# Two v stages become one: half of the second token tile's experts by fetched rows and VectorE additions, on one Trainium2 core

## The reference, cut to what matters

```python
def blk(args):                      # hx: tokens x 2048, e: expert numbers, gt: gates
    hx, e, gt = args
    act = jax.nn.gelu(jnp.einsum('nd,nhkd->nhk', hx, expert_u[e]), approximate=False)
    return jnp.einsum('nhk,nhkd->nd', gt * act, expert_v[e])
```

## Time and profile before

| | |
|---|---|
| time, median of 3 runs (lowest, highest) | 3488.04 us (3487.63, 3488.38) |
| profiled execution, span from first to last instruction | 3487.5 us |
| busy: PE, PEld, DVE, ACT, POOL | 99%, 83%, 63%, 51%, 10% |
| moved by DMA | 638.58 MB, mean 183 GB/s |
| granted TensorE clock, mean | 0.998 |

### The profile page before, as it was taken

How to read it: one execution, slowest core, us unless ns; L and a number is a source line. 1 busy time by engine, 2 the same in 40 slices (tenths; PEclk the granted TensorE clock), 3 DMA queues, 4 the chain that set the end, 5 groups by cost and what they waited for, 6 DMA issues and landing times. The chain is left out here.

```text
span 3487.5 us, 50169 instructions
## 1 busy us (share of the span) xinstructions
PE 3450.4 (99%) x20098; PEld 2893.0 (83%) x20098; DVE 2194.8 (63%) x2937; ACT 1766.6 (51%) x2613; POOL 347.2 (10%) x215
## 2 busy tenths in 40 slices
PE   8999999999999999999999999999999999999999
PEld 7777777787999998888888888887788877788887
DVE  4777765765666686555555565555788885555454
ACT  5563444334444785444444444444655654444863
POOL 0000000000499100000000000000122210000000
PEclk9999999999999999999999999999999999999999
DMA  6554533565445555555555666555543435455444
GB/s 235 203 198 156 174 138 130 187 232 212 161 183 182 174 168 183 215 190 185 191 213 184 240 231 228 189 185 180 191 148 138 148 140 202 168 194 190 145 150 164
DMA packets 111214, 638.58 MB, mean 183 GB/s; under 512 B 17770, under 2 KB 23690, under 8 KB 39224
## 3 DMA queue, kind: packets, MB, share of 16 engines
q1 hardware_dynamic: 106696, 622.98, 50.0%
q0 software_dynamic: 4336, 13.14, 1.2%
HBM read 611.10 MB, written 21.54 MB: 181 GB/s over the span
## 5 line engine op out<-in xcount | busy, mean ns | idle before, releaser
L222 DVE TENSOR_TENSOR lo_w<-ring,hi_w 128x1024 fp32r<-128x1024 f32 x500 | 612.4, 1225 | 862.7 <-ACT hi_w L216 854.2
L216 ACT CAST hi_w<-ring 128x1024 fp32r<-128x1024 f32 x540 | 567.1, 1050 | 946.3 <-DMA ring<-in_wstream 920.6
L224 DVE TENSOR_TENSOR lo_w<-ring,hi_w 128x1024 fp32r<-128x1024 f32 x500 | 612.4, 1225 | 0.0
L217 ACT CAST hi_w<-ring 128x1024 fp32r<-128x1024 f32 x540 | 564.4, 1045 | 0.0
L639 PE MATMUL PS<-hi_w,both_x 128*128 128x512 f32 (+2 forms) x1520 | 500.2, 399 | 4.9 <-DVE RKV L1651 3.0
L2074 PE MATMUL PS<-hi_w,hi_g 128*128 128x512 f32 x1024 | 404.0, 395 | 2.0 <-issue 2.0
L2667 PE MATMUL PS<-hi_w,both_x 128*128 128x512 f32 x1232 | 401.3, 401 | 4.1 <-PEq L1968 1.9
L2074 PE MATMUL PS<-lo_w,hi_g 128*128 128x512 f32 x1024 | 403.4, 394 | 0.0
L2074 PE MATMUL PS<-hi_w,lo_g 128*128 128x512 f32 x1024 | 403.2, 394 | 0.0
L2048 PE MATMUL PS<-both_x,hi_w 128*128 128x256 f32 x2176 | 390.5, 281 | 3.1 <-POOL lo_w L224 3.1
L639 PEld LDWEIGHTS PS<-hi_w,both_x 128*128 128x128 f32 x1520 | 285.2, 189 | 78.3 <-issue 12.3
(11 more groups left out here) (579 smaller groups left out, 5272.4 us busy)
## 6 DMA issues: line engine op xcount, KB each, us to landing
ring<-in_wstream SPq DMA_DIRECT2D x540, 1024.0 KB, 4.8
other_G<-staged SPq DMA_DIRECT2D x32, 256.0 KB, 6.0
hot<-other_G SPq DMA_DIRECT2D x8, 1024.0 KB, 7.0
gates_dram<-gst POOLq DMA_DIRECT2D x8, 512.0 KB, 4.6
x_dram<-x SPq DMA_DIRECT2D x2, 2048.0 KB, 11.8
x<-x_dram SPq DMA_DIRECT2D x2, 2048.0 KB, 9.3
prev<-RKV POOLq DMA_DIRECT2D x6, 508.0 KB, 5.1
x<-in_x SPq DMA_DIRECT2D x4, 512.0 KB, 8.9
```

Source lines behind the costliest of these rows:

```text
L216: a.copy(hi_w[s][:, 0:HALF], ring[s][:, 0:HALF]).then_inc(S(f"hi{s}"), 1)
L217: a.copy(hi_w[s][:, HALF:UNIT], ring[s][:, HALF:UNIT]).then_inc(S(f"hi{s}"), 1)
L222: v.tensor_tensor(lo_w[s][:, 0:HALF], ring[s][:, 0:HALF], hi_w[s][:, 0:HALF].bitcast(F32), ALU.subtract)
L224: v.tensor_tensor(lo_w[s][:, HALF:UNIT], ring[s][:, HALF:UNIT], hi_w[s][:, HALF:UNIT].bitcast(F32), ALU.subtract)\
```

## The change

The order of the stages becomes u of the experts from 64 on (called u_b: both tiles, unpaired), u of those below 64 (u_a, unpaired), then one v stage of 128 units. Its first 64 units are the experts from 64 on, for both tiles, as before. Its last 64 are those below 64, for the first token tile alone: 12 matmuls of 512 columns each in place of 24.

Note that the diff's `v_expert(p)` calls the last 64 units sparse, and that `HK + i` in the layout of the stream are the experts from 64 on.

For the second tile the experts below 64 go another way. In 128 steps, one per pick, GpSimd fetches by indirect DMA for each of the 128 tokens the v row of that pick (`fetch`: 128 x 2048 float32 into one of three, later four, later three buffers), and VectorE adds it to x of that tile with its weight in one scalar_tensor_tensor (`add_row`). Picks of experts from 64 on are out of the bounds of the fetch and are skipped; their weight is 0. The weight is the gate times the gelu, which GpSimd fetches one word per token from DRAM (`cell`: 128 indirect DMAs of 128 words, into a raw array that starts at 0; VectorE multiplies 32 of them at a time, `weigh`, at ticks 9, 12, 36 and 38 of u_a). So the gelus of u_b (whose name in DRAM is act_dram) are stored unit by unit by SyncE (`keep_act`, 128 KB each). Additions 0 to 53 stand in u_a, one per unit from unit 10; 54 to 127 in the first 61 units of v.

What moves besides. lo_w: GpSimd makes it for all 64 units of u_b, VectorE for all of u_a, and in v GpSimd for even and VectorE for odd units. G: VectorE copies one half of each burst to GG (`copied`) in place of copy and product, ScalarE stages the other half for the first tile only (16 of 32). In u_a VectorE multiplies each unit's gelu into GG (`times_a`). The gelus of the first tile's last 64 v units are loaded from DRAM (`load_act`, six slots, 64 KB each), as is a table of G for them (tab_b, 4 MB in one DMA before the first v unit), and VectorE multiplies them (`times_b`, with a strided read of the table). GG's layout changes, so that one unit's 256 values are contiguous. `u_sum`, `product`, `product_back`, `late` go, and so do the save and reload of x in the middle and four of the final eight additions to x (the second tile's four stand after the 64th v unit). The u parts of both halves are unchanged in what they compute.

The diff, cut ("..." marks what is left out):

```diff
-STREAM = [("w_in", 19), ("br_b", 2), ("br_a", 2), ("w_out", 4), ("wq", 4), ("u0", 16), ("v0", 16), ("u1", 16), ("v1", 16),
+STREAM = [("w_in", 19), ("br_b", 2), ("br_a", 2), ("w_out", 4), ("wq", 4), ("u_b", 16), ("u_a", 16), ("v", 32),
           ("a_in", 16), ("a_out", 4), ("kv", 8), ("b_in", 8), ("b_out", 4)]
...
+HK = PK // 2
+def v_expert(p):
+    return p >= HK, p % HK
...
+    act_dram = scratch("act_dram", (HK, P, T))
...
+    rows = {"x0": x[:, 0, :], "h1": lanes(hot1), "h2": lanes(hot2), "g0": GG[:, 0:8, :].rearrange("p i t -> p (i t)")}
+    x1 = x[:, 1, :]
...
+    ADD0, ADDS_U = 10, HK - 10
+    ADDS_V = PK - ADDS_U
+    SPAN_V = LAST_A - 2
+    adds_u = lambda i: [i - ADD0] if i >= ADD0 else []
+    adds_v = lambda p: list(range(ADDS_U + ADDS_V * min(p, SPAN_V) // SPAN_V, ADDS_U + ADDS_V * min(p + 1, SPAN_V) // SPAN_V))
...
+            with sp.Fori(0, STEADY // SLOTS) as j:
+                for s in range(SLOTS):
+                    sp.wait_ge(S("unit_used"), j * SLOTS + (W0 + s + 1))
+                    sp.dma_start(ring[s][:], wst[ds(j * SLOTS + (W0 + SLOTS + s), 1)].rearrange("a p f -> p (a f)"))\
+                        .then_inc(S(f"landed{s}"), 16)
+                    sp.wait_ge(S("gelu_free"), j * SLOTS + (s + 5))
+                    sp.dma_start(act_dram[ds(j * SLOTS + s, 1)].rearrange("a p t -> p (a t)"), act_early[:, s, :])\
+                        .then_inc(S(f"act_out{s}"), 16)
...
+            refill(GROUP["u_a"], 1)
+            sp.wait_ge(S("G"), NB)
+            for s in range(SLOTS):
+                sp.wait_ge(S(f"act_out{s}"), 16 * (HK // SLOTS))
+            for k in range(AHEAD):
+                load_act(k)
+            refill(GROUP["u_a"] + 1, HK // SLOTS - 1)
             for p in range(2):
...
+                sp.wait_ge(S(f"other_out{p}"), 8 * NB0)
+            sp.dma_start(tab_b, other_G).then_inc(S("tab_in"), 16)
+            for p in range(VB):
+                refill_unit(VB + p)
+                sparse, k = v_expert(p)
+                if sparse and k + AHEAD < HK:
+                    load_act(k + AHEAD)
...
-                    if paired:
-                        nc.tensor.matmul(PS[:, s, :].rearrange("p (a c) -> p a c", a=2), hi_w[s][:, k * P:(k + 1) * P], both_x[:, :, k, :],
-                                         start=k == 0, stop=False)
-                        m = nc.tensor.matmul(PS[:, s, 0:T], lo_w[s][:, k * P:(k + 1) * P], hi_x[:, k, :], start=False, stop=k == KC - 1)
-                        continue
...
+            def v_half(g, s, last=False):
+                t.wait_ge(S(f"lo{s}"), g + (GROUP["v"] + 1))
+                t.wait_ge(S("g_lo"), g * 4 + (s + 1))
+                for c in range(4):
+                    m = v_products(g, s, 0, c, False, last)
+                    if last and c < 3:
                         m.then_inc(S("v_bank"), 1)
...
+            for w in range(2 * HK):
+                for j in at_unit(w):
+                    if j < NB0:
+                        stage(j)
+                    if j + 2 < NB:
+                        gate(j + 2)
...
+                if SLOTS <= w < HK + SLOTS:
+                    a.wait_ge(S(f"act_out{w % SLOTS}"), 16 * (w // SLOTS))
+                elif w >= HK + SLOTS:
+                    a.wait_ge(S("gg_mul"), w - HK - SLOTS + 1)
+                a.wait_ge(S("unit_used"), W0 + w + 1)
+                a.activation(act_stage(w), PS[:, w % SLOTS, 0:T], ACT.Gelu).then_inc(S("gelu_free"), 1)
...
+            for p in range(VB):
+                if p + 2 < VB:
+                    high(p + 2)
+                hi(VB + p + SLOTS - 1)
...
-            for w in range(AT_UNIT[0]):
+            def fetch(s):
+                n = row_of[s]
+                if row_before[s] >= 0:
+                    g.wait_ge(S("added"), row_before[s] + 1)
+                elif n == "g0":
+                    g.wait_ge(S("unit_used"), W0 + VB + 8)
+                elif n in ("h1", "h2"):
+                    g.wait_ge(S("G"), NB)
+                g.indirect_dma_start(rows[n], None, dram["v_rows"], bass.IndirectOffsetOnAxis(ap=row_at[:, s:s + 1], axis=0),
+                                     bounds_check=HK * P - 1, oob_is_err=False).then_inc(S(f"row_{n}"), 16)
+            def cell(s):
+                g.indirect_dma_start(raw[:, s:s + 1], None, act_cells, bass.IndirectOffsetOnAxis(ap=cell_at[:, s:s + 1], axis=0),
+                                     bounds_check=HK * P * T - 1, oob_is_err=False).then_inc(S(f"cells{s // CELLS}"), 16)
+            def lo(w):
                 split_lo(g, (W0 + w) // SLOTS, w % SLOTS)
+            for w in range(HK):
+                lo(w)
+                if w == 48:
+                    g.wait_ge(S("row_at"), 1)
+                    fetch(0)
+            for s in (1, 2):
+                fetch(s)
+            for s in range(SLOTS):
+                g.wait_ge(S(f"act_out{s}"), 16 * (HK // SLOTS))
+            for s in range(2 * CELLS):
+                cell(s)
+            for i in range(ADD0, HK):
+                for s in fetches(i):
+                    fetch(s)
+                at = 2 * CELLS + 4 * (i - ADD0)
+                for s in range(at, min(at + 4, PK)):
+                    cell(s)
+            lo(VB)
+            lo(VB + 2)
+            for p in range(VB):
+                for s in fetches(HK + p):
+                    fetch(s)
+                if p % 2 and p + SLOTS - 1 < VB:
+                    lo(VB + p + SLOTS - 1)
...
-                if AT_UNIT[0] <= w < 4 * HK + SLOTS:
+                if HK <= w < VB or VB <= w < 2 * VB and w % 2 or 2 * VB <= w < 2 * VB + SLOTS:
                     split_lo(v, (W0 + w) // SLOTS, w % SLOTS)
...
+            def copied(j):
+                if j == 0:
+                    for s in range(SLOTS):
+                        v.wait_ge(S(f"act_out{s}"), 16 * (AT_UNIT[0] // SLOTS))
                 v.wait_ge(S("G"), j + 1)
-                v.wait_ge(S("gelu_free"), m + 4)
                 b = 4 + 2 * (j % 2)
                 got = PS[:, b:b + 2, :].rearrange("p b (n i) -> p (b n) i", i=PK)
-                o = GG[:, 8 * j:8 * j + 8, 0:m]
-                v.tensor_copy(late_, got[:, :, m:HK])
-                v.tensor_tensor(o, o, got[:, :, 0:m], ALU.mult).then_inc(S("G_product"), 1)
...
+                v.tensor_copy(GG[:].rearrange("p i t -> p t i")[:, 8 * j:8 * j + 8, :], got[:, :, HK:PK])
+                v.drain().then_inc(S("G_copy"), 1)
...
+            def add_row(s):
+                n = row_of[s]
+                if s == 0:
+                    v.wait_ge(S("x_again"), 16)
+                v.wait_ge(S(f"row_{n}"), 16 * row_turn[s])
+                v.scalar_tensor_tensor(out=x1, in0=rows[n], scalar=weight[:, s:s + 1], in1=x1, op0=ALU.mult, op1=ALU.add)
+                v.drain().then_inc(S("added"), 1)
+            def times_a(i):
+                v.wait_ge(S("gelu_free"), HK + i + 5)
+                v.tensor_tensor(GG[:, i, :], GG[:, i, :], act_stage(HK + i), ALU.mult).then_inc(S("gg_mul"), 1)
+            def times_b(k):
                 if k == 0:
+                    v.wait_ge(S("tab_in"), 16)
+                v.wait_ge(S(f"act_in{k % AHEAD}"), 16 * (k // AHEAD) + 16)
+                o = act_b[:, k % AHEAD, :]
+                v.tensor_tensor(o, o, tab_b[:, :, k], ALU.mult).then_inc(S("gb_mul"), 1)
+            def low(p):
+                sparse, k = v_expert(p)
+                v.wait_ge(S("g_hi"), p + 1)
+                src, w = (act_b[:, k % AHEAD, :], P) if sparse else (GG[:, k, :], T)
+                v.tensor_tensor(lo_g[:, p % SLOTS, 0:w], src, hi_g[:, p % SLOTS, 0:w].bitcast(F32), ALU.subtract).then_inc(S("g_lo"), 1)
...
+            for i in range(ROUTED, HK):
+                for j in at_unit(i):
+                    copied(j)
+                    if j + 2 < NB:
+                        build(j + 2)
+            lo(HK)
+            lo(HK + 1)
+            for i in range(HK):
+                lo(HK + i + SLOTS - 2)
+                if i:
+                    times_a(i - 1)
+                if i in (9, 12, 36, 38):
+                    weigh((9, 12, 36, 38).index(i))
+                for s in adds_u(i):
+                    add_row(s)
...
+            times_a(HK - 1)
+            v.drain()
+            for p in range(VB):
+                if p + 3 < VB and v_expert(p + 3)[0]:
+                    times_b(v_expert(p + 3)[1])
+                    v.drain()
+                if p + 2 < VB:
+                    low(p + 2)
+                if p < VB - 1:
+                    lo(VB + p + SLOTS - 1)
+                for s in adds_v(p):
+                    add_row(s)
```

398 lines of the change are left out of this document (186 added, 212 removed).

## The result

The changed kernel takes 3589.51 us (median of 4 runs, 3587.56 to 3592.66) against 3488.21 us (3487.63 to 3496.78) for the kernel before, a ratio of 1.0284 with a 95% interval of 1.027 to 1.0299: 101 us slower where 27 us less were forecast, and outside the range of 3370 to 3550. Nothing in the sum hangs on it.

What follows compares the result with a forecast made beforehand. TensorE, busy 99% of the span, was taken as the bound. Terms: v stages 41 us gained, first u stage 9 lost, second u stage 5 lost, the rest 0; -27 on 3488.0 gave 3461 us, range 3370 to 3550.

Steps and rivals of the forecast that it cites:

- part 7, the cells: Second u stage: 128 single-cell indirect DMAs plus fetches on GpSimd, 0.94 us each, cost 0; upper bound 130 us.
- Part 2, half units: The 64 one-tile v units: 3.75 us each, 240 us in all; bounds 3.4 and 4.4 us.
- The ring of 14.8 us: Half units: refill, cast, lo_w with holds, then TensorE take 14.8 us per turn of four units, a quarter being 3.7.
- Part 3, whole units: Whole v units with additions: GpSimd's lo_w holds VectorE off, 6.75 us per unit, 428 us; bounds 5.54 and 7.5.
- The rival without any hold: v stage: additions not held off, whole units 5.54 us, total 3358, or 3379 to 3388; chance 0.15.
- Part 4, bursts: First u stage: GpSimd's lo_w and VectorE's one-hots hold each other off, 9 us lost; bounds 0 and 35 us.
- Part 6: Transfers: row fetches, 4 MB table at the first v unit and activation loads cost 0; table up to 5 us.
- Parts 1 and 5: v units: TensorE alone would save 177 us; second u stage: unpaired units at 5.69 us, 5 us lost.
- Part 8: Ends of stages: final additions into x split 4 and 4, reload and save of x go; cost 0.
- the third rival: Half units: TensorE's granted clock falls to the 0.51 level, 4.4 us per unit, 42 us more, 3503; chance 0.08.
- the second rival: Second u stage: GpSimd's indirect DMAs become the bound; at c = 1.5 us each, 57 us, 3518; chance 0.25.
- the forecast's own case: Whole kernel, no rival true: 3461 us, own range about 3425 to 3505; chance 0.50.

Runs made afterwards that it cites:

- Edit 1: Changed kernel with 32 single cells first, then two per unit (before 64, then four), weights formed at units 9, 40, 50, 62: 3527.7 us, ratio 1.0105.
- edit 2: Changed kernel with VectorE making lo_w for all 128 v units and GpSimd for none: 3434.9 us, ratio 0.9834.

## Why the prediction was wrong, step by step

- **The step that failed: part 7, the cells, put at 0.** The price per indirect DMA was taken from the earlier trace rows, 0.94 us, as busy time of a direct DMA. It is 0.99 busy and 1.30 from start to start, as the rows above show, 1.43 in the mean of the 64 in a row and 1.6 in the ticks, where one in each lies beside an addition. "At 0.94: 0" became 62 us. The rival had it right, with its place, both of its terms and its break-even (1.29 us). With the measured prices the part's own formulas give 65 x 1.43 - 69 = 24 us for the 64 in a row (22 measured, in one unit) and 16 x (8.0 - 5.69) = 37 for the ticks (about 41). Edit 1 removes the cause and gives 62 us back. What no term had is that TensorE's clock falls with its waits, 17 of the 62 us.
- **Part 2, half units: 36 us.** The ring of 14.8 us counted holds on lo_w, 5.6 us for GpSimd's two halves, and left out the other chain, product with the table (times_b), hi_g, lo_g, where each small VectorE operation can wait for a whole one of GpSimd's. Two such, a lo_g that took 0.29 us in the run of edit 2 and a times_b of 0.37, from the changed kernel's timeline of the half units:

```profile
2300.82 1.61 DVE L2517 TENSOR_TENSOR lo_g<-R,hi_g 128x128 fp32r<-128x128 f32 x1 [0.81 <-ACT hi_g L2276]
...
2309.00 2.50 DVE L2510 TENSOR_TENSOR R<-R,both_x 128x128 f32<-128x128 f32 x1
```

  ScalarE waited 41.7 us for that product from 2250 to 2440. In the half units TensorE waited 53.4 us for lo_g and 12.0 for GpSimd's lo_w, where the prediction had named lo_w alone. That this chain is what sets the 4.32 us is read from these waits; the run of edit 2 shows that all holds together cost 78 us. A share of it is the clock: at a granted 0.88 a half unit kept TensorE busy for 143.81/44 = 3.27 us (44 units in 190 us), at 0.99 for 183.42/61.3 = 2.99. With VectorE alone at it, a half unit takes 198.6/64 = 3.10 us, under the lower bound of 3.4 us. That bound had GpSimd's 4.7 us for both halves of lo_w in the ring, and VectorE needs 2.4; besides, the sum without a hold-off is 13.9 us and not 13.7.
- **Part 3, whole units: right in kind, 17 us short.** Outside two single waits a unit took 6.70 us for 6.75. The two, 10 and 8 us longer than the others, were in no term: one is the fetch that waits for its buffer in GG with a low part behind it in GpSimd's queue, the other the hold of 10.96 us. Where the text said the hold would show was wrong: additions keep their 2.35 us, and not "3 us and over"; a subtraction begun during a fetch takes 6.2. That scalar_tensor_tensor meets the hold, which the text took from the Trainium skill ("SBUF — State Buffer", "Who interferes with whom"), the trace bears out: beside one in the whole units GpSimd's subtraction took 3.83 us, not 2.36. That page's inference that making descriptors is not held off by such operations does not carry over to these fetches: 2.21 us in the mean among additions, 1.04 with the additions cut to 8 columns. A fetch reads its list of indices from SBUF besides, and no run tells which of the two is held. The rival without any hold (3358 to 3388) falls.
- **Part 4, bursts: 12 us for 9**, by the mechanism named, the one-hots at 1.95 to 2.02 us instead of 1.22.
- **Part 6: the table at 0 held**, the load of 4 MB did no harm; the 9 us at the first v unit are holds, which the sum had in no term. Bytes were no limit in the changed kernel, as said; once the holds are gone they are, in the half units, at 363 GB/s over 190 us and not at the 419 of 8 us in the earlier trace rows.
- **Parts 1 and 5** held: cells spread, the second u stage took 362.6 us for 364. Part 8 was not tested by itself.
- **The signs of being wrong.** Three were named, and all three came: additions of 2.35 us beside GpSimd's work, a period over 6 us in the second u stage (426.6/64 = 6.7), and a granted clock under 1.00. The first is no sign against the hold, which falls on the subtractions. The clock did not fall to 0.5 for the half units as the third rival had it; it was 0.88 there, 0.95 in the second u stage and 0.96 in the whole units.
- **The range** ended at 3550: it took the second rival to c = 1.7 alone, and half and whole units at their own upper ends (4.1 and 7.2) only in the forecast's own case. All terms erred to the same side, since all rest on one engine's queue; bounds that share a cause have to be added, not taken one at a time. Added, the forecast's own upper ends (22 + 27 + 11) give 3521, and with the 62 us of the cells 3583.

## What to carry to other kernels

Price an instruction of a queue from start to start, with what runs beside it, and when a second engine is given half of a job, add its whole time to the engine that it holds off. Here VectorE alone did both shares faster (3.10 us per half unit) than VectorE and GpSimd together (4.32). Work that must be fetched piecewise has to fit the queue in every tick: two cells beside a fetch did (5.65 us a unit), four did not, whether 32 or 64 had gone first. And look in each queue for a wait on a buffer with other engines' work behind it.

## What was not expected of the hardware

- An indirect DMA costs GpSimd the same 0.99 us for 128 words and for up to 128 rows of 8 KB; the next starts 1.30 us after it. Of the 77 that overlapped an addition on VectorE 59 took 1.5 to 3.1 us, the others 0.99 to 1.17.
- The hold between GpSimd and VectorE is not fair. Usually their operations alternate, as in the earlier trace rows; a VectorE subtraction that begins at the end of an indirect DMA, with GpSimd's subtractions next in its queue, waits for two of them (6.23 us), once for four (10.96 us).
- On some chips TensorE's instructions come 0.7 to 1.4 us apart while indirect DMAs are issued back to back, in the first turns of a new loop: 3625.9 against 3588.9 us with the same kernel.
- After waits TensorE works at a lower granted clock: the same 3072 matmuls kept it busy for 361.8 us in a stage without waits (clock 1.00) and for 378.8 us in one with 48 us of them (0.95).
